# Three projections of a gated encoder layer: block by block, or as seven jobs of seven half-size products

## What is computed

```python
h = _rmsnorm(x, norm_mix_g)
q_a, k_a, v_a, u_p, q_x = split(h @ w_in)                 # 1024 -> 1792
y_attn = _window_attention(q_a, k_a, v_a, attn_sinks)     # 8 heads, window 128
y_pool = _multiscale_pool(u_p, w_pool, pool_scale)
y_mem = _memory_attention(q_x, mem_k, mem_v)              # 256 memory tokens
gates = sigmoid(h @ w_gate + b_gate)                      # 1024 -> 3 x 1024
merged = (gates[:, :, 0] * (y_attn @ w_branch_attn) + gates[:, :, 1] * (y_pool @ w_branch_pool)
          + gates[:, :, 2] * (y_mem @ w_branch_mem))
x = x + merged @ w_out                                    # "out", 1024 x 1024
hm = _rmsnorm(x, norm_mlp_g)
x = x + square(relu(hm @ w_up)) @ w_down                  # "up" 1024 x 4096, "down" 4096 x 1024
return _rmsnorm(x, norm_final_g)
```

## Time and profile before

| | us |
|---|---|
| median of 3 runs | 2945.35 (2944.4 to 2946.05) |
| the profiled execution | 2946.49 |
| its span, first to last instruction | 2944.8 |
| PE busy | 2890.6 (98%) |
| DVE busy | 1350.5 (46%) |
| ACT busy | 961.5 (33%) |
| POOL busy | 195.3 (7%) |
| transfers | 293.99 MB, mean 100 GB/s |

### The profile page before, as it was taken

How to read it: one execution, slowest core, us unless ns; L and a number is a source line. 1 busy time by engine, 2 the same in 40 slices (tenths; PEclk the granted TensorE clock), 3 DMA queues, 4 the chain that set the end, 5 groups by cost and what they waited for, 6 DMA issues and landing times.

```text
span 2944.8 us, 35670 instructions
## 1 busy us (share of the span) xinstructions
PE 2890.6 (98%) x13481; PEld 2391.0 (81%) x13481; DVE 1350.5 (46%) x1625; ACT 961.5 (33%) x1425; POOL 195.3 (7%) x191
## 2 busy tenths in 40 slices
PE   8999999999999999999999999999999999999998
PEld 7788888888778888888877888888887888888886
DVE  4643344445364245444446334544444632454444
ACT  5542332222353233212245323322224432422223
POOL 0101110000010111000001011000000001100000
PEclk9999999999999999999999999999999999999999
DMA  5123333332322342333232234223323222432332
GB/s 187 61 83 97 121 122 100 100 98 88 101 62 86 100 157 86 100 100 100 86 102 69 79 100 157 91 95 100 100 86 102 69 86 93 157 99 88 99 100 86
DMA packets 290347, 293.99 MB, mean 100 GB/s; under 512 B 9704, under 2 KB 285212, under 8 KB 290204
## 3 DMA queue, kind: packets, MB, share of 16 engines
q1 hardware_dynamic: 287900, 283.71, 30.3%
q0 software_dynamic: 2304, 8.39, 0.7%
HBM read 283.67 MB, written 8.39 MB: 99 GB/s over the span
## 4 chain that ended last, share of the span: by engine, by line
PE 90%; issue 5%; DVE 2%; POOL 1%; ACT 1%; DMA 0%; DVEq 0%; POOLq 0%; ACTq 0%
PE ps L993 29%; PE ps L995 28%; PE ps L994 28%; PE ps L998 1%; POOL sq_sum L971 1%; PE ps L1145 1%; PE ps L1128 1%; PE ps L1116 1%; PE ps L1089 0%; ACT sq L357 0%; DVE u_lo L806 0%; DVE scores L733 0%; DVE out_tm L897 0%; DVE scores L715 0%; DVE h_lo L656 0%
## 5 line engine op out<-in xcount | busy, mean ns | idle before, releaser
L993 PE MATMUL ps<-h_hi,w_hi 128*128 128x512 f32 x2240 | 885.2, 395 | 12.7 <-issue 12.7
L995 PE MATMUL ps<-h_hi,w_lo 128*128 128x512 f32 x2240 | 874.7, 390 | 0.0
L994 PE MATMUL ps<-h_lo,w_hi 128*128 128x512 f32 x2240 | 874.4, 390 | 0.0
L615 DVE TENSOR_TENSOR w_lo<-stage,w_hi 128x2048 fp32r<-128x2048 f32 (+1 forms) x269 | 559.6, 2080 | 641.6 <-ACT w_hi L357 641.6
L357 ACT ACTIVATE w_hi<-stage 128x2048 fp32r<-128x2048 f32 (+2 forms) x287 | 485.1, 1693 | 526.0 <-PE ps L995 524.6
L993 PE MATMUL ps<-u_hi,w_hi 128*128 128x512 f32 x1280 | 501.0, 391 | 5.5 <-DVE u_lo L806 5.5
L993 PEld LDWEIGHTS ps<-h_hi,w_hi 128*128 128x128 f32 x2240 | 422.3, 189 | 101.9 <-issue 14.3
L995 PE MATMUL ps<-u_hi,w_lo 128*128 128x512 f32 x1280 | 498.4, 389 | 0.0
L994 PE MATMUL ps<-u_lo,w_hi 128*128 128x512 f32 x1280 | 498.1, 389 | 0.0
L995 PEld LDWEIGHTS ps<-h_hi,w_lo 128*128 128x128 f32 x2240 | 422.1, 188 | 88.8
L994 PEld LDWEIGHTS ps<-h_lo,w_hi 128*128 128x128 f32 x2240 | 422.6, 189 | 86.7 <-issue 1.0
(11 more groups left out here) (153 smaller groups left out, 1837.9 us busy)
## 6 DMA issues: line engine op xcount, KB each, us to landing
stage<-in_w_up SPq DMA_DIRECT2D x128, 512.0 KB, 4.7
stage<-in_w_down SPq DMA_DIRECT2D x128, 512.0 KB, 4.0
stage<-in_w_gate SPq DMA_DIRECT2D x96, 512.0 KB, 4.5
stage<-in_w_in SPq DMA_DIRECT2D x60, 512.0 KB, 4.8
stage<-in_w_out SPq DMA_DIRECT2D x32, 512.0 KB, 4.1
x_tm<-in_x SPq DMA_DIRECT2D x5, 2048.0 KB, 9.6
stage<-in_w_branch_attn SPq DMA_DIRECT2D x32, 256.0 KB, 4.0
stage<-in_w_branch_pool SPq DMA_DIRECT2D x32, 256.0 KB, 3.0
```

The source lines that it names most:

```text
L615: v.tensor_tensor(w_lo[:, slot, 0:kt, :], stage[:, slot, 0:kt, :], w_hi[:, slot, 0:kt, :].bitcast(F32), ALU.subtract).then_inc(lo_done, 1)
L993: mm(dst, wh, xh, start=first, stop=False)
L994: mm(dst, wh, xl, start=False, stop=False)
L995: return mm(dst, wl, xh, start=False, stop=last)
```

## The change

The out, up and down projections leave the block loop. What is left in a block ends with the merge stage: POOL's queue stores the merged sum in a DRAM tensor (`mrg_d`, feature-major), and the next block's rows (`x_next`, loaded and normed during the merge stage) are transposed all at once. After the loop follow seven **jobs**, written out flat in 72 **quartets**:

- job 0, out (8 quartets): C = merged^T w_out, resident operand `w_out`, pieces of 256 tokens;
- jobs 1 and 2, up (16 quartets each): resident operand 1024 tokens of the normed rows, pieces of 256 columns of `w_up`;
- jobs 3 to 6, down (8 quartets each): resident operand a 1024x1024 slab of `w_down`, pieces of 256 tokens of the squared up result.

A quartet is the product of one 1024x256 piece with the resident 1024x1024 operand. Both are cut in 2x2 quarters and multiplied by the scheme of Winograd: four sums of piece quarters (S1 to S4, POOL, `s_sums`), four sums of resident quarters (T1 to T4, DVE and POOL, once a job), **seven** half-size products in the order A11, S2, S1, S3, A12, A22, S4 (12 matmuls of 512 columns each: 4 k-steps of 3), and seven additions on DVE that give four 128x512 tiles of C. Products use six PSUM banks in turn. `s_hi`/`s_lo` are a ring of six slots, and `piece_f`, the piece in float32, is a **single** buffer. The seven resident entries (`res_hi`, `res_lo`, 128x2048 each) are a single buffer too: an entry of the next job is written when the last quartet of this job has used it.

Between jobs everything goes through DRAM. The out and down jobs add their tiles on POOL (`add_tile`) to rows of 256 tokens (`rows_tm`, two slots, 1 MB each), which SP loads and stores (`rows_d`) in every such quartet; the up jobs store relu(x)^2 tiles to `up_d`. In job 0 the rows are normed, transposed by PE (`rows_across`, 16 transposes a quartet) and stored as `ht_d`; in job 6 they are normed and stored as the output. The doubling of the gated branches' results is undone earlier (`scale=0.5` on y), so that no scaling is left at the end.

```diff
@@ constants @@
-W_MERGE, W_OUT, W_MLP = 16, 32, 36
-PIECES = 68
+W_MERGE = 16
+PIECES = 32
+N_OUT, N_UP, N_DOWN = 8, 16, 8
+FIRST = [0, 8, 24, 40, 48, 56, 64]
+NQT = 72
+SLOTS = 6
+PROD = 7
+A11, S2, S1, S3, A12, A22, S4 = range(PROD)
@@ SP, block @@
-                for j in range(4):
-                    load(j % 2, w_outv[:, :, j * PC:(j + 1) * PC], lo0 + (W_OUT + j))
...
+                    if j == 0:
+                        sp.wait_ge(tile_done, t0 + G_MERGE)
+                        sp.dma_start(x_next[:], x_rows[:, bass.ds(row_n, TT), :]).then_inc(x_ld, 16)
@@ SP, jobs @@
+            for n in range(NQT + 1):
+                if squares(n - 1):
+                    store_up(n - 1, 3, c12, 0, 1)
+                if adds_rows(n - 1) and not is_final(n - 1):
+                    sp.wait_ge(row_add, 4 * row_quartets(n))
+                    store_rows(n - 1, rows_v)
+                if n + 1 < NQT:
+                    sp.wait_ge(s_lo_done, PROD * n + 6)
+                    sp.wait_ge(s_done, 4 * n + 4)
+                    load_piece(n + 1)
+                if is_final(n - 1):
+                    sp.wait_ge(fin_rdy, n - FIRST[6])
+                    store_rows(n - 1, out_v)
...
+                if adds_rows(n + 1) and not 0 < n < N_OUT:
...
+                    sp.wait_ge(row_st[row_slot(m)], 16 * slot_uses(m))
+                    load_rows(m)
+                if n < NQT and starts(n + 2):
...
+                    for i in range(3):
+                        load_quarter(j, i)
...
+                if n + 1 < NQT and starts(n + 1):
+                    sp.wait_ge(prod, PROD * n + A12 + 1)
+                    load_b21(job_of(n + 1))
...
@@ ACT, jobs @@
+            for n in range(NQT):
...
+                take_p1(n)
+                s_split(n, 6)
+                if first:
+                    r_split(j, 4)
+                    r_split(j, 6)
+                if last:
+                    r_split(j + 1, 0)
+                if has_norm(n - 1):
+                    row_squares(n - 1)
+                s_split(n + 1, 0)
+                if first:
+                    r_split(j, 5)
+                s_split(n + 1, 1)
...
@@ DVE, jobs @@
+            for n in range(NQT):
+                j, first, last = job_of(n), starts(n), starts(n + 1) and n + 1 < NQT
+                if first:
+                    r_low(j, 3)
+                s_low(n, 6)
+                take_u2(n)
+                if last:
+                    r_low(j + 1, 0)
+                    t1(j + 1)
...
+                if has_norm(n - 1):
+                    row_var(n - 1)
+                s_low(n + 1, 0)
+                if has_norm(n - 1):
+                    scale_tile(n - 1)
+                if first:
+                    r_low(j, 6)
+                    r_low(j, 4)
+                    r_low(j, 5)
+                take_c22(n)
+                if last:
+                    t2(j + 1)
+                relu_sq(n, C22)
+                s_low(n + 1, 1)
+                s_low(n + 1, 2)
+                take_c11(n)
+                relu_sq(n, C11)
+                if last:
+                    r_low(j + 1, 1)
+                take_ht(n - 1, 0)
+                s_low(n + 1, 3)
+                take_c21(n)
+                relu_sq(n, C21)
+                take_ht(n - 1, 1)
+                s_low(n + 1, 4)
+                if last:
+                    r_low(j + 1, 2)
+                take_c12(n)
+                relu_sq(n, C12)
+                s_low(n + 1, 5)
@@ POOL, jobs @@
+            for n in range(NQT):
+                add_tile(n - 1, C12, 0, 1)
+                if first:
+                    t4(j)
+                row_rms(n - 1)
+                s_sums(n + 1, S1)
+                s_sums(n + 1, S2)
+                s_sums(n + 1, S3)
+                if last:
+                    t3(j + 1)
+                add_tile(n, C22, 1, 1)
+                s_sums(n + 1, S4)
+                add_tile(n, C11, 0, 0)
+                add_tile(n, C21, 1, 0)
@@ PE, block end @@
+                pe.wait_ge(xn_rdy, b + 3)
+                for k in range(KT):
...
+                        last = transpose(ring[:, q % 4, t * P:(t + 1) * P], x_next[:, t, k * P:(k + 1) * P])
@@ PE, jobs @@
+            for n in range(NQT):
+                for i in range(PROD):
+                    pe.wait_ge(s_lo_done, PROD * n + i + 1)
+                    if starts(n):
+                        pe.wait_ge(r_lo_done, PROD * j + R_LO_ORDER.index(i) + 1)
+                    if i == S4:
+                        pe.wait_ge(ev_act, n + 1)
+                    elif n:
+                        pe.wait_ge(ev_dve, 7 * (n - 1) + FREED[i + 1])
+                    for k in range(4):
+                        last = product(dst, s_hi[:, slot, k, :], s_lo[:, slot, k, :], res_hi[:, i, k, :], res_lo[:, i, k, :],
+                                       k == 0, k == 3)
+                    last.then_inc(prod, 1)
+                    if i in (A12, A22):
+                        rows_across(n - 1, i - A12)
```

817 lines of the change are left out of this document (499 added, 318 removed).

## The result

The changed kernel took **2997.6 us** (median of 4 runs, 2997.25 to 3000.8) against 2945.7 us (2944.4 to 2947.09) before: ratio 1.0179, 95% interval 1.0161 to 1.0196. It is **1.8% slower**. Forecast were 2868 us, range 2790 to 2940. The profiled execution took 3000.8 us, with a span of 2999.1.

What follows compares the result with a forecast made beforehand. PE was taken to bound the kernel. Front parts 1285.3, block ends 28.5, start 60, 71 quartets 1351.1, out job 30, switches 80, row loop 5, clock 12, end 15 give 2866.9 us span, so 2868 us, range 2790 to 2940.

Steps and rivals of the forecast that it cites:

- PE's saving: In the jobs: 6048 matmuls in place of 6912, 196 us less, at 19.03 us of PE a quartet.
- rival 4: In the product matmuls: fewer, but at 0.235 rather than 0.2266 us each, 51 us more, 2919 us; chance 0.03.
- Front parts and block ends: In the blocks: front parts stay 1285.3 us, x_next load costs 0; three block ends add 28.5 us.
- First quartet: Start of job 0, behind the last block: first quartet ends at 57 us, with disturbance 60.
- End: After the last products: addition, POOL add, four squares, pow, scaling and a 1 MB store take 15 us.
- Keeping up inside a quartet: Mid-job: DVE 9.7 or 12.4, ACT 5.1, POOL 5.3 or 10.6 us, all under 19.03, so hidden.
- Row loop: Down jobs 3 to 5: store, load and POOL's sums and adds form a ring of 20.2 us, costing 5 us.
- Job switches: At the six switches: PE waits for DVE's queue, 13 us at five and 15 at one, 80 in all.
- rival 2: At the switches: deeper waits, T3 and T4 block DVE's long rests; 24 us each, not 15; 2932 us; chance 0.15.
- Clock: At the six switches: matmuls behind PE's gaps run at a slower clock, 2 us each, 12 in all.
- Out job: Job 0, quartets 1 to 7: scaling and transposes chain through PE, 4.3 us over each, 30 in all.
- rival 3: Down jobs: each DVE rest blocks POOL for 0.69 us, ring 23.5 us, 88 in place of 5, 2961; chance 0.07.

Runs made afterwards that it cites:

- e1: The changed kernel with SP issuing the next piece's load ahead of the store of the last quartet's rows: 2937.8 us.
- e4: The changed kernel with POOL's row additions writing only 8 of 512 columns, all waits, loads and stores kept: 2926.9 us.
- e7: The changed kernel with DVE's rest of each piece's quarter, from the eleventh quartet on, taking its second input from an idle PSUM bank: 2935.4 us.
- e8: The changed kernel with the out job's scaling of the rows done by ACT instead of DVE: 2978.3 us.
- c4: The changed kernel with load ahead of row store, resident's rests ahead of the next piece's, T3 and T4 on DVE, out job's scaling on ACT: 2876.6 us.
- c3: The changed kernel with the piece's load ahead of the row store and the resident's rests ahead of the next piece's: 2913.9 us.

## Why the prediction was wrong

The sum was 132.2 us short of the measured span (2866.9 against 2999.1). Point by point, in its order:

- **PE's saving**: right. 6048 product matmuls, up intervals of 19.04 us (19.03 said), no sign of rival 4.
- **Front parts and block ends**: right. Matmuls of block 1 start at 360.95, 8.6 us after the transposes' start at 352.31 (9.5 said, answering to the earlier trace rows); the last block's transposes start at 1312.14, where the sum has 1313.8. The x_next load cost nothing that can be told: the three front parts take 310.5, 311.6 and 311.8 us, 311.4, 310.9 and 310.7 before.
- **First quartet**: its end is 69.2 us behind that (at 1381.35, the second quartet's first matmul) instead of 60. **End**: the last addition (c12) starts at 2984.26, 14.8 us before the span's end; 15 said.
- **Keeping up inside a quartet**: the step from "all lie under 19.03" to "hidden" held in the up jobs; in down jobs no engine's total was over 19.04 either, but the ring through them was.
- **Row loop**: the mechanism was right and almost its size. Ring forecast 20.2, measured 21.0: issue 0.59 for 0.4, landing 7.62 for 7.7 (its 2.8 for a second MB is 2.6 at 399 GB/s), POOL 12.79 for 10.6 + 1.5. The term that was mis-sized is the ring, "with 0.3 for each of some 5 encounters the ring is 20.2", and not the slack of 6.5 us behind it. By PE's first matmuls job 3 has four quartets of 19.0 to 19.3 us, then 21.6, 22.5 and 21.0: of 7 x 1.96 us 8.2 are lost, so 5.5 were slack. With 21.0 the prediction's own formula gives 22 us for the three jobs; measured are 24.2 by PE's first matmuls and 34.8 by `u2`, for 5. The step from 20.2 to 21.0 counts in full because the slack was used up. Job 6 was put at nothing and has 9.3 by `u2`, of which PE lost 1.8. It is another ring, in which the load already stands ahead of the store: landing 5.4 us behind the issue, then on DVE the first rest, the scaling (4.54 us for two, 1.28 for one where POOL is idle) and the rests up to the sixth, for which the next load waits, 21.1 in all. e1 leaves it as it is, e4 and e7 bring it to 19.0.
- **Job switches**: the step that failed most, 163.7 for 92. The queue of DVE was laid out with the durations of the earlier trace rows, which are those of an engine left alone, plus 2.5 for "about ten" encounters. One pair of rests behind T3 cost 5.3 of extra, one rest behind T4 4.4, and the rest of entries 4 and 5 5.55 for 4.6. In all it is 17.1 us each at the switches into jobs 4 to 6, 6.7 into jobs 2 and 3 and 5.1 into job 1, where the sum has 2.5 each. The six add up to 70 us, and the term is 72 short; the two need not match item by item, since some of it falls where DVE waits anyway and the clock is in the term too. T3 and T4 themselves were put at 5.3 from four POOL operations and took 6.08 and 5.97 on the mean, their own waits for DVE included (4.5 the shortest). The prediction had this as a part of rival 2 ("T3 and T4 block DVE's long rests outright") and put 24 us a switch on it; it was 27.3. The price of 0.3 from the earlier trace rows is what POOL lost beside one 128x512 product; it was then used for both engines, though the earlier trace rows has DVE losing 0.76 on four elements and 0.96 on 512. The addition at 109.11 in the earlier trace rows ends at 110.02, together with this row of POOL in the trace of before (108.93 + 1.07):

```profile
108.93 1.07 POOL L946 TENSOR_TENSOR win_sum<-u_pad 128x527 f32<-128x527 f32 x1
```

So the old trace did show that DVE waits for the end of POOL's operation, and with it that the price grows with that operation's length. The fifth product as the worst place was only half right: a second gap of the same size (11.47) stood behind T3, where the sum had waits of 0.3 and 1.0.
- **Clock**: 2 us a switch said. Behind the gap of 11.47 us six matmuls ran at a granted clock of 0.50 (1.2 GHz), 0.2 us more each, and nine behind the next gap of 1.79: some 3 us. Twelve more behind the gap of 11.52 us ahead of the fifth product ran at that clock, so it is 5.5 us at this switch. In the first quartets of jobs 1 to 6 129 matmuls do, 27 us in all, for 12 in the sum. Some of them are followed by a wait that would have come anyway, so the cost is 27 us at most. Right in kind, too small in size.
- **Out job**: 55.5 over the seven intervals for 30, of which 7.4 are the wait ahead of the first quartet's fifth product, which the 60 covers. Mis-sized term: the scaling, 2 x 0.75 from the earlier trace rows, took 3.45 beside POOL's work; e8 gives 2.5 us a quartet for it. The scaling reads one tensor from SBUF, not two, so "both inputs in SBUF" does not cover it; no run here varied its inputs.

**The rivals.** What came is rival 2 at the switches (164 where it has 146) and, in kind, rival 3: its ring of 23.5 was too long, 21.0 was enough. Their prices added to the forecast, 64 + 93, give 3025, 0.9% above the result; each alone gives 2932 or 2961. They were weighed as alternatives, with 0.15 and 0.07, though they rest on one cause. With the lock-out given, both come true together, and that is the error of the chances and of the range. The trace of before, in which POOL was busy for 7%, had few encounters, but those of the earlier trace rows already spoke for it.

**What each part is worth.** From e1 to c4, 123 of the 263 us of excess come back by four moves without changing any arithmetic: the load order (55 of excess), the resident's rests first (27 more, c3), T3 and T4 on DVE (15), scaling on ACT (26, of which 19.5 in the out job). c4's excess is 140.5, near the 127 forecast, though by other parts: the switches still have 109 (92 forecast), job 6 10.9 (0), the out job 20.6 (30). About the switches it is shown that PE waits there for DVE's queue, in both intervals; how much of c4's 109 us is the lock and how much the plain amount of work was not separated.

## What to carry to other kernels

When a change loads an engine that idled, durations of its partner from the old trace are those of an idle neighbour: price every pair of DVE and POOL operations on SBUF that can overlap with the length of the longer one, and put long ones (2.3 us and more) on one engine. A ring through a single buffer that comes out within a microsecond or two of the bound is to be taken as over it: order the load ahead of the store. If two rivals rest on one mechanism, give the mechanism the chance and add their prices.

## What the hardware showed that was not expected

- DVE 0.69 and POOL 1.29 us (128x512, all operands in SBUF) beside each other take 1.18 and 1.74; with one DVE input from PSUM they take 0.68 and 1.29.
- The loser waits for the whole of the other's instruction: 5.06 us for a rest of 0.69 behind a POOL operation of 2048 elements. Cutting such operations into four lets DVE in after each, but the four then took 8.87 us for 6.08 (T3) and 7.51 for 5.97 (T4) on the mean.
- The lock holds POOL too. In e4 a POOL addition of 8 columns takes 0.19 to 0.20 us in 17 cases, none of them beside a DVE operation with SBUF inputs, and 0.58 us or more in the 143 others: with a DVE rest of 0.69 beside it, it ends 0.06 us behind that rest.
- ACT scaled 128x1024 by a value a row in 1.14 us beside POOL's work; DVE took 1.75, with one tensor input from SBUF (0.75 on the mean in the trace of before, where POOL was busy for 7%).
